# Scatter of the pair that went ahead, moved between the two gate and up products of an expert pair

## The chip, the cores and the metric

The kernel runs on one core of one Trainium2 chip. The metric is the device time of one execution in microseconds; three executions of the kernel before gave 1489.64, 1482.80 and 1488.08 us, median 1488.08 us.

## The reference

256 tokens of width 1024, all in float32, go through one layer of a first model (attention with rotary positions, a spatial gating unit, attention over 256 memory rows, a mixture of experts) and two layers of a second (stick-breaking attention and retention, each followed by a mixture of experts). The change lies in the three mixtures of experts alone. Each of them computes, cut to what matters:

```python
for e in range(16):
    he = silu(t @ w_gate[e]) * (t @ w_up[e])       # 256 x 1024 by 1024 x 512, twice
    y = y + combine[:, e:e + 1] * (he @ w_down[e]) # 512 x 1024
```

`combine` is zero for all but two experts of a token, so a kernel may compute for each expert only the tokens that chose it.

## The kernel before, in words

Five engines run their own programs and meet at semaphores. The matrix work is TensorE's, written in the order in which it is executed. In what follows the three mixtures of experts are called layers 0, 1 and 2.

**Tiling of a layer.** Each expert gets 64 slots (`CAP`) for tokens. Four experts form a quad: `gather_quad` fills their 256 slots by products with a 0/1 matrix `SELQ` that DVE makes. Two experts form a pair, worked on together: the even one sits in rows 0 to 63, the odd one in rows 64 to 127. A layer has 8 pairs, p = 0 to 7, p = 2q + k for quad q and half k. Pairs 0, 1, 6 and 7 are written out; pairs 2 to 5 are two rounds of a loop over q.

**A pair on TensorE (function `pair`, from line 927).** In this order:
1. `gate_up` for the even expert (a = 0): 16 products of 64 x 512 with `w_gate` and `w_up`; then the same for the odd expert (a = 1). Each waits for its two weight panels (`landed`), and for `ye`, the count of finished output halves of the pair ahead.
2. k = 0: `turn_pair_slots` twice, which turns `SELQ` for both pairs of the quad. k = 1: first half of `gather_quad` for the next quad.
3. `turn_h`: four transposes of the hidden rows `HH`, after ACT's silu (line 1533) and DVE's product (line 2195) for the odd expert (`h`). ACT copies the turned rows into `HT` (line 1563), which `ht` counts.
4. `down_half` for output columns 0 to 511, the other half of `gather_quad` where k = 1, `down_half` for columns 512 to 1023.
5. `more`: if an expert has over 64 tokens, a further block of 64 with products of its own (lines 994 and on). Its branch is passed twice in each pair.

**The scatter.** After `down_half`, ACT and DVE weight an output half and split it into a high and a low part, `YH` and `YL` (`ye` counts them). `scatter_before(h)` of the next pair adds column half h of the pair that went ahead into four accumulators: 4 products of 128 x 512 with the turned selection `SELTS`. A pair has two, so 8 products. It waits for `ye` and for `swt`, ACT's copies of the turned selection. The second one counts up `moe_scat`; before `YH`, `YL` and one of the selections are written anew, ACT and DVE wait for that. In the kernel before, where k = 0, `scatter_before(0)` stands between the turns of the slots and `turn_h`, and `scatter_before(1)` behind `turn_h`; where k = 1, both stand behind `turn_h`. Pair 0 of a layer has none (`first`), and the last pair's own output is scattered at the end of the layer.

**The weights.** Each expert has three panels of 2 MB (`w_gate`, `w_up`, `w_down`). A ring of six slots holds one pair's six panels: `ring_lo` for the even expert, `ring_hi` for the odd one. SyncE issues the loads (`load_expert`, line 1211) for the next pair, in this order: gate and up of the even expert, gate and up of the odd one, down of the even one, down of the odd one. Each waits until the slot has been read: gate and up until that expert's `gate_up` has ended, down until the pair's `down_half` has. All loads go through one queue.

Of the kernel before, what the change touches and what calls it, by code (L numbers as in the profile page):

```python
# [100 lines left out]
def build(nc, A, out, stop, final_ready):  # L101
# [7 lines left out]
    def S(name):  # L109
        if name not in sems:  # L110
            sems[name] = ctx.enter_context(nc.semaphore(name))
        return sems[name]
# [304 lines left out]
    def _(pe):  # L417
# [341 lines left out]
        def moe(L):  # L759
# [167 lines left out]
            def pair(q, k, first=False, final=False):  # L927
# [18 lines left out]
                if k == 0 and not first:  # L946
                    wait_moe(pe, L, "xe_a", 2 * q + 2)
                    wait_moe(pe, L, "xe_v", 2 * q + 2)
                for a in range(2):
                    if not first:  # L950
                        wait_moe(pe, L, "ye", 2 * p - 1 + a)
                    for j in range(2):
                        pe.wait_ge(landed[s[a][j]], 16 * p + at[a][j])
                    lo = P * k + CAP * a
                    gate_up(banks[a], lambda c: XE[:, c, lo:lo + CAP], wg[a], wu[a], S("moe_gu"), a == 0,
                            chunks_in if first and a == 0 else None)
                    if first and a == 0 and L:
                        pe.wait_ge(S("diag"), 2 * L)
                        for h in range(2):
                            ins = mm(ps[:, (B_XG, B_TR)[h], :], cst(C_ONES), GB[:, h * 512:(h + 1) * 512], True, True)  # L960
                        ins.then_inc(S("gate_sum"), 1)
                if k == 0:
                    if first:
                        pe.wait_ge(S("turner_in"), 2 * L + 2)
                        if L:
                            pe.wait_ge(S("gate_in"), L)
                    turn_pair_slots(0)
                    turn_pair_slots(1)
                    if not first:
                        scatter_before(0)  # L970
                elif not final:
                    wait_moe(pe, L, "sel", q + 2)
                    wait_moe(pe, L, "swt", 2 * q + 2)
                    wait_moe(pe, L, "ws", 2 * q + 2)
                    gather_quad(0)
                wait_moe(pe, L, "h", 2 * p + 2)
                turn_h(banks[0])
                if k == 1:
                    scatter_before(0)
                if not first:  # L980
                    scatter_before(1).then_inc(S("moe_scat"), 1)
                wait_moe(pe, L, "ht", p + 1)
                for a in range(2):
                    pe.wait_ge(landed[s[a][2]], 16 * p + at[a][2])
# [1608 lines left out]
```

## Time and profile before

| | us |
|---|---|
| median of three runs | 1488.08 |
| lowest and highest | 1482.80, 1489.64 |
| the profiled execution's own time | 1482.80 |
| its span, first to last instruction | 1480.9 |
| TensorE matmul busy | 1320.8 (89%) |
| DVE, ACT, POOL busy | 581.3, 431.7, 410.2 |
| DMA bytes, mean rate | 448.04 MB, 303 GB/s |
| mean granted TensorE clock | 0.968 of full speed |

A timeline row gives the start of a group of instructions within the span, how long it lasted, engine, line, tiles, shape and count, and in brackets how long the engine sat idle before it and what ended that. "issue" means that the profile shows no other instruction that it waited for. All products are made in one helper, line 419; which product a row is, its tiles tell: `ring_lo` or `ring_hi` with `Z` x32 is a `gate_up` of the even or the odd expert (the trace has two entries for each of the 16 products), `TURN,SELQ` the turns of slots, `YHS,SELTS` and `YLS,SELTS` the scatter, line 884 `turn_h`, and `ring_lo` alternating with `ring_hi` a `down_half`. The layers lie at about 289 to 521 us (layer 0), 697 to 962 us (layer 1) and 1214 to 1468 us (layer 2) of the span.

### The profile page before, as it was taken

How to read it: one execution, taken by the hardware profiler on the slowest of the kernel's cores; microseconds unless marked ns; L12 is line 12 of the kernel's file. 1: busy time of each engine (PE TensorE's matmuls, PEld its weight loads, DVE VectorE, ACT ScalarE, POOL GpSimd, SP SyncE). 2: the span in 40 equal slices, each digit the busy share in tenths (PEclk: the TensorE clock that was granted, in tenths of full speed). 3: DMA queues.
4: the chain of work that ended last, by engine and by line, in shares of the span. 5: the costliest groups of instructions: out<-in, count | busy, mean ns of one | idle time of the engine just before them, and what ended most of it. 6: DMA issues, size and time to landing. Idle time of an engine off the chain costs nothing.

```text
span 1480.9 us, 20887 instructions
## 1 busy us (share of the span) xinstructions
PE 1320.8 (89%) x7694; PEld 815.7 (55%) x7695; DVE 581.3 (39%) x1234; ACT 431.7 (29%) x693; POOL 410.2 (28%) x190
## 2 busy tenths in 40 slices
PE   7999987889899889998789799789997979889975
PEld 6886775534334389766234334279886853333422
DVE  5598543612112162447214222279007062322224
ACT  4554433211111146443111111145435331111110
POOL 5892643100000067151000000069964710000000
PEclk9999999999999999999899999999999999999998
DMA  7664566999999975518589999976544479999953
GB/s 285 215 201 173 186 228 231 393 402 426 426 428 428 391 283 183 190 58 338 231 344 420 426 422 428 397 269 235 191 150 191 170 321 412 422 416 420 427 221 126
DMA packets 89628, 448.04 MB, mean 303 GB/s; under 512 B 7804, under 2 KB 9768, under 8 KB 70952
## 3 DMA queue, kind: packets, MB, share of 16 engines
q1 hardware_dynamic: 85856, 445.87, 75.4%
q8 instruction: 79, 1.29, 0.4%
q10 hardware_dynamic: 3656, 0.57, 0.3%
q14 instruction: 37, 0.30, 0.1%
HBM read 445.38 MB, written 1.05 MB: 301 GB/s over the span
## 4 chain that ended last, share of the span: by engine, by line
PE 65%; DMA 15%; DVE 9%; issue 4%; POOL 3%; ACT 3%; ACTq 0%; SPq 0%; DVEq 0%; POOLq 0%
PE ps L419 63%; DMA ring_hi<-in_moe_w_up 10%; DMA ring_hi<-in_w_up 3%; POOL WLO L2528 3%; DMA ring_hi<-in_ada_w 1%; ACT WHI L1326 1%; DVE Z L1944 1%; DVE Z L1932 1%; DVE Z L1945 1%; DVE Z L1943 1%; DMA ring_lo<-in_w_ckv 1%; PE ps L884 1%; DMA ring_lo<-in_ret_w_in 1%; DMA ring_lo<-in_w_out 1%; POOL RS L2497 1%
## 5 line engine op out<-in xcount | busy, mean ns | idle before, releaser
L2528 POOL TENSOR_TENSOR WLO<-ring_lo,WHI 128x1024 fp32r<-128x1024 f32 (+1 forms) x154 | 379.3, 2485 | 702.6 <-ACT WHI L1326 700.7
L419 PE MATMUL ps<-ring_hi,Z 128*64 128x512 f32 x1248 | 375.4, 616 | 25.3 <-DMA ring_hi<-in_moe_w_up 14.4
L419 PE MATMUL ps<-ring_lo,Z 128*64 128x512 f32 x1152 | 350.6, 613 | 33.6 <-issue 24.3
L419 PEld LDWEIGHTS ps<-ring_lo,Z 128*64 128x64 f32 x1152 | 111.0, 141 | 248.2 <-issue 234.1
L1326 ACT ACTIVATE WHI<-ring_lo 128x1024 fp32r<-128x1024 f32 (+1 forms) x160 | 165.5, 1048 | 214.1 <-PE ps L419 177.3
L419 PEld LDWEIGHTS ps<-ring_hi,Z 128*64 128x64 f32 x1248 | 119.6, 142 | 153.7 <-issue 147.5
L2195 DVE TENSOR_TENSOR Z<-ps,Z 64x512 f32<-64x512 f32 x48 | 33.1, 689 | 357.4 <-ACT Z L1533 354.2
L1533 ACT ACTIVATE Z<-ps 64x512 f32<-64x512 f32 x48 | 28.4, 591 | 370.4 <-PE ps L419 357.6
L419 PE MATMUL ps<-WHI,HTH 128*128 128x512 f32 x320 | 126.8, 396 | 7.2 <-POOL WLO L2528 3.2
L419 PE MATMUL ps<-WLO,HTH 128*128 128x512 f32 x320 | 125.1, 391 | 0.0
L419 PE MATMUL ps<-WHI,HTL 128*128 128x512 f32 x320 | 125.1, 391 | 0.0
L2497 POOL TENSOR_TENSOR RS<-MS,NEGH 128x1 f32<-128x1 f32 (+2 forms) x26 | 22.2, 856 | 357.8 <-DVE MS L1781 298.7
L419 PE MATMUL ps<-HTH,WHI 128*128 128x256 f32 x320 | 92.2, 288 | 6.6 <-POOL WLO L2528 4.0
L419 PE MATMUL ps<-HTL,WHI 128*128 128x256 f32 x320 | 91.2, 285 | 0.0
L419 PE MATMUL ps<-HTH,WLO 128*128 128x256 f32 x320 | 91.1, 285 | 0.0
L419 PEld LDWEIGHTS ps<-WHI,HTH 128*128 128x128 f32 x320 | 60.5, 189 | 22.5 <-issue 6.3
L419 PEld LDWEIGHTS ps<-WHI,HTL 128*128 128x128 f32 x320 | 60.4, 189 | 12.9
L419 PEld LDWEIGHTS ps<-WLO,HTH 128*128 128x128 f32 x320 | 60.5, 189 | 11.9
L419 PEld LDWEIGHTS ps<-HTH,WHI 128*128 128x128 f32 x320 | 62.1, 194 | 8.4 <-issue 5.0
L419 PEld LDWEIGHTS ps<-HTL,WHI 128*128 128x128 f32 x320 | 62.1, 194 | 0.0
L419 PEld LDWEIGHTS ps<-HTH,WLO 128*128 128x128 f32 x320 | 62.1, 194 | 0.0
L419 PE MATMUL ps<-SELQ,XSPLIT 128*128 128x256 f32 x288 | 50.7, 311 | 5.7 <-DVE SELQ L2144 5.7
(299 smaller groups left out, 1719.2 us busy)
## 6 DMA issues: line engine op xcount, KB each, us to landing
ring_lo<-in_ada_w SPq DMA_DIRECT2D x22, 2048.0 KB, 8.1
ring_lo<-in_moe_w_gate SPq DMA_DIRECT2D x16, 2048.0 KB, 12.1
ring_lo<-in_moe_w_up SPq DMA_DIRECT2D x16, 2048.0 KB, 16.5
ring_lo<-in_moe_w_down SPq DMA_DIRECT2D x16, 2048.0 KB, 12.6
ring_hi<-in_moe_w_gate SPq DMA_DIRECT2D x16, 2048.0 KB, 13.6
ring_hi<-in_moe_w_up SPq DMA_DIRECT2D x16, 2048.0 KB, 18.5
ring_hi<-in_moe_w_down SPq DMA_DIRECT2D x16, 2048.0 KB, 16.9
ring_lo<-in_ret_w_in SPq DMA_DIRECT2D x12, 2048.0 KB, 8.1
```

The source lines that it names most:

```text
L419: return nc.tensor.matmul(o, l, r, start=start, stop=stop, skip_group_check=True)
L884: ins = nc.tensor.transpose(ps[:, bank, c * P:(c + 1) * P], by4[:, c, :], ident)
L1326: nc.scalar.activation(WHI[:, q, 0:size], slot(r)[:, q * size:(q + 1) * size], Copy).then_inc(S("hi_split"), 1)
L1533: nc.scalar.activation(SG[r, :], ps[CAP - CAP * a:P - CAP * a, bank, :], ACT.Silu).then_inc(S("moe_sg"), 1)
L1932: ins = V.tensor_tensor(qk4[:, t, h], qk4[:, t, h], gain, ALU.mult)
L1943: V.tensor_tensor(t1, x0, c1, ALU.mult)
L1944: link(V.tensor_tensor(t2, x1, c2, ALU.mult))
L1945: link(V.tensor_tensor(o, t1, t2, op))
L2195: V.tensor_tensor(HH[r, :], ps[r, bank, :], SG[r, :], ALU.mult).then_inc(S("moe_h"), 1)
L2497: nc.gpsimd.tensor_tensor(RS[:, par, at:at + width], MS[:, par, at:at + width], NEGH[:, 0:width], ALU.pow).then_inc(S("rstd"), 1)
L2528: nc.gpsimd.tensor_tensor(WLO[:, q, 0:size], slot(r)[:, q * size:(q + 1) * size], WHI[:, q, 0:size].bitcast(F32), ALU.subtract).then_inc(S ...
```

## The change

Both calls of `scatter_before` now stand between the `gate_up` of the even and of the odd expert, in each pair but the first. Nothing is added or taken away.

```diff
                 for a in range(2):
+                    if a and not first:
+                        scatter_before(0)
+                        scatter_before(1).then_inc(S("moe_scat"), 1)
                     if not first:
                         wait_moe(pe, L, "ye", 2 * p - 1 + a)
                     for j in range(2):
...
                     turn_pair_slots(0)
                     turn_pair_slots(1)
-                    if not first:
-                        scatter_before(0)
                 elif not final:
...
                 wait_moe(pe, L, "h", 2 * p + 2)
                 turn_h(banks[0])
-                if k == 1:
-                    scatter_before(0)
-                if not first:
-                    scatter_before(1).then_inc(S("moe_scat"), 1)
                 wait_moe(pe, L, "ht", p + 1)
```

TensorE's program in the loop, k = 0 (pairs 2 and 4), before; `landed3` and `landed4` are the odd expert's gate and up panels, `CST,Z` is `turn_h`:

```order
L419 MATMUL ps<-ring_lo,Z 64x512 x15
L953 REGISTER_ALU [waits moe_ye]
L419 MATMUL ps<-ring_hi,Z 64x512 [waits landed4,landed3]
L419 MATMUL ps<-ring_hi,Z 64x512 x15
L419 MATMUL ps<-TURN,SELQ 128x160 x4
L419 MATMUL ps<-YHS,SELTS 128x512 [waits moe_swt,moe_ye]
...
L884 MATMUL ps<-CST,Z 128x128 [waits moe_h]
L884 MATMUL ps<-CST,Z 128x128 x3
L419 MATMUL ps<-YHS,SELTS 128x512 [waits moe_swt,moe_ye]
...
L419 MATMUL ps<-ring_lo,Z 64x512 [waits landed5,landed1,moe_ht]
```

The same place after the change:

```order
L419 MATMUL ps<-ring_lo,Z 64x512 x15
L419 MATMUL ps<-YHS,SELTS 128x512 [waits moe_swt,moe_ye]
...
L956 REGISTER_ALU [waits moe_ye]
L419 MATMUL ps<-ring_hi,Z 64x512 [waits landed4,landed3]
L419 MATMUL ps<-ring_hi,Z 64x512 x15
L419 MATMUL ps<-TURN,SELQ 128x160 x4
L884 MATMUL ps<-CST,Z 128x128 [waits moe_h]
L884 MATMUL ps<-CST,Z 128x128 x3
L419 MATMUL ps<-ring_lo,Z 64x512 [waits landed5,landed1,moe_ht]
```

All eight scatter products now stand ahead of the odd expert's `gate_up`, and none stands beside the waits for `h` and `ht`.

TensorE's program of pair 1, k = 1 (its `gather_quad` is `SELQ,XSPLIT`), before:

```order
L419 MATMUL ps<-ring_hi,Z 64x512 [waits landed4,landed3,moe_ye]
...
L419 MATMUL ps<-SELQ,XSPLIT 128x256 [waits moe_ws,moe_swt,moe_sel]
...
L884 MATMUL ps<-CST,Z 128x128 [waits moe_h]
L884 MATMUL ps<-CST,Z 128x128 x3
L419 MATMUL ps<-YHS,SELTS 128x512 [waits moe_swt,moe_ye]
...
L419 MATMUL ps<-ring_lo,Z 64x512 [waits landed5,landed1,moe_ht]
```

And after the change:

```order
L419 MATMUL ps<-YHS,SELTS 128x512 [waits moe_swt,moe_ye]
...
L419 MATMUL ps<-ring_hi,Z 64x512 [waits landed4,landed3,moe_ye]
...
L419 MATMUL ps<-SELQ,XSPLIT 128x256 [waits moe_ws,moe_swt,moe_sel]
...
L884 MATMUL ps<-CST,Z 128x128 [waits moe_h]
L884 MATMUL ps<-CST,Z 128x128 x3
L419 MATMUL ps<-ring_lo,Z 64x512 [waits landed5,landed1,moe_ht]
```

Here the gather still stands beside the wait for `h`; beside the wait for `ht` nothing is left.

## Rows read from the trace of the kernel before

**Rows 1.** The page's chain of waits, shares of the span by engine.
```profile
PE 65%; DMA 15%; DVE 9%; issue 4%; POOL 3%; ACT 3%; ACTq 0%; SPq 0%; DVEq 0%; POOLq 0%
```

**Rows 2.** A stretch of layer 0: length, busy per engine, clock, DMA share, GB/s.
```profile
298.00:508.00 210.00, 190.04 (x886) 79.20 (x882) 39.47 (x116) 29.98 (x56) 0.00 (x0) 0.97 1.00 424
```

**Rows 3.** Timeline of TensorE, layer 0, pair 0, which has no scatter.
```profile
303.17 0.68 PE L419 MATMUL ps<-TURN,SELQ 128*128 128x160 f32 x4
304.67 0.75 PE L884 MATMUL ps<-CST,Z 128*128 128x128 f32 x4 [0.82 <-DVE Z L2195]
306.10 0.64 PE L419 MATMUL ps<-ring_lo,Z 128*64 128x512 f32 x1 [0.69 <-ACT Z L1563]
```

**Rows 4.** Timeline of TensorE, layer 0, pair 2 (k = 0).
```profile
359.87 0.68 PE L419 MATMUL ps<-TURN,SELQ 128*128 128x160 f32 x4
...
362.96 0.64 PE L419 MATMUL ps<-ring_lo,Z 128*64 128x512 f32 x1
```

**Rows 5.** Timeline of TensorE, layer 0, pair 5 (k = 1).
```profile
449.80 0.65 PE L884 MATMUL ps<-CST,Z 128*128 128x128 f32 x4
450.20 0.48 PE L419 MATMUL ps<-YHS,SELTS 128*128 128x512 f32 x1
...
452.21 0.64 PE L419 MATMUL ps<-ring_lo,Z 128*64 128x512 f32 x1
```

**Rows 6.** Timeline of ACT, the same pair: the copy of the turned rows.
```profile
450.72 0.60 ACT L1563 ACTIVATE Z<-ps 128x512 f32<-128x512 f32 x1
```

**Rows 7.** Timeline of TensorE, layer 2, pair 7, the last.
```profile
1454.52 0.75 PE L884 MATMUL ps<-CST,Z 128*128 128x128 f32 x4 [1.43 <-DVE Z L2195]
...
1457.04 0.64 PE L419 MATMUL ps<-ring_lo,Z 128*64 128x512 f32 x1
```

**Rows 8.** Timeline of TensorE, layer 2: starts of the products of pairs 2, 3, 5 and 6.
```profile
1272.20 8.79 PE L419 MATMUL ps<-ring_lo,Z 128*64 128x512 f32 x32 [4.69 <-issue]
...
1301.59 9.79 PE L419 MATMUL ps<-ring_lo,Z 128*64 128x512 f32 x32 [3.54 <-issue]
...
1365.02 7.09 PE L419 MATMUL ps<-ring_hi,Z 128*64 128x512 f32 x32 [1.06 <-DMA ring_hi<-in_moe_w_up]
...
1386.20 7.09 PE L419 MATMUL ps<-ring_lo,Z 128*64 128x512 f32 x32 [0.39 <-issue]
1394.96 7.09 PE L419 MATMUL ps<-ring_hi,Z 128*64 128x512 f32 x32 [1.67 <-DMA ring_hi<-in_moe_w_up]
```

**Rows 9.** Timeline of TensorE, layer 0: products of pairs 5 and 7.
```profile
439.06 8.78 PE L419 MATMUL ps<-ring_hi,Z 128*64 128x512 f32 x32 [2.79 <-DMA ring_hi<-in_w_up]
...
488.01 7.09 PE L419 MATMUL ps<-ring_lo,Z 128*64 128x512 f32 x32 [1.95 <-DMA ring_lo<-in_w_up]
...
497.90 8.78 PE L419 MATMUL ps<-ring_hi,Z 128*64 128x512 f32 x32 [2.80 <-DMA ring_hi<-in_w_up]
```

**Rows 10.** Timeline of TensorE, layer 1: products of pairs 3, 5, 6 and 7.
```profile
819.03 8.73 PE L419 MATMUL ps<-ring_hi,Z 128*64 128x512 f32 x32 [2.71 <-DMA ring_hi<-in_moe_w_up]
...
880.04 7.09 PE L419 MATMUL ps<-ring_hi,Z 128*64 128x512 f32 x32 [0.94 <-DMA ring_hi<-in_moe_w_up]
...
909.41 7.09 PE L419 MATMUL ps<-ring_hi,Z 128*64 128x512 f32 x32 [1.09 <-DMA ring_hi<-in_moe_w_up]
...
928.98 7.09 PE L419 MATMUL ps<-ring_lo,Z 128*64 128x512 f32 x32 [2.39 <-DVE YLS L2209]
938.75 8.60 PE L419 MATMUL ps<-ring_hi,Z 128*64 128x512 f32 x32 [2.68 <-DMA ring_hi<-in_moe_w_up]
```

**Rows 11.** Timeline of SyncE: issue of layer 1's last panel, start and duration of the issue.
```profile
927.12 0.33 SPq L1211 DMA_DIRECT2D ring_hi<-in_moe_w_down  x1
```

**Rows 12.** DMA issues, window 926.6 to 928: KB each, us from issue to landing.
```profile
ring_hi<-in_moe_w_down SPq DMA_DIRECT2D x1, 2048.0 KB, 22.9
```

**Rows 13.** Timeline of TensorE, layer 2, the further block of pair 6.
```profile
1416.15 1.13 PE L860 MATMUL ps<-CST,XROWS 128*128 128x128 f32 x4 [1.58 <-ACT XROWS L1583]
1419.48 8.87 PE L419 MATMUL ps<-ring_hi,Z 128*64 128x512 f32 x32 [2.20 <-DVE Z L2186]
```

## The prediction

> **What bounds the kernel now.** I read the chain of waits first. It is TensorE for 65% of the span and DMA for 15% [rows 1]. So the order on TensorE counts, but a part of its time in the layers of experts is waiting for weights. Next I read stretches of the layers. From 298 to 508 us the DMA engines are busy all the time, at 424 GB/s [rows 2]. A pair's six panels are 12.58 MB; at 424 GB/s that is 29.7 us per pair. The third view is TensorE's timeline in a pair. There the two work at nearly the same pace: TensorE waits 0.9 to 2.8 us for a panel in some pairs [rows 8 to 10] and not at all in the others. A step that TensorE gains or loses in such a layer is therefore taken up by the next wait for a panel, as long as there is one, and reaches the end of the layer only behind the last such wait. I cost the change in each pair first, and then walk through the waits of each layer.
>
> **What the scatter costs where it now stands.** Eight products start at 450.20 and the next thing starts at 452.21 [rows 5]: 2.0 us with the change of weights, of which I count 1.9. Between the two `gate_up` nothing hides it, unless the odd expert's panel is late. The scatter itself waits for nothing there: its `ye` was reached before or soon after the pair began, and its `swt` in the pair ahead.
>
> **What it gives back where it stood.** Its old place hid waits, and that cover is now gone.
> - k = 0, pairs 2, 4, 6. From the turns of the slots to the first down product takes 3.09 us with the scatter [rows 4]. Pair 0 has no scatter, and needs 2.93 us: it sits idle 0.82 us for DVE's product and 0.69 us for ACT's copy instead [rows 3]. So the scatter was hidden but for 0.16 us. Taken with 1.9 us ahead, such a pair gets 1.7 us longer.
> - k = 1 with a gather, pairs 1, 3, 5. The gather covers the wait for DVE. `turn_h` starts at 449.80, the down product at 452.21, 2.41 us later [rows 5]. ACT's copy ended at 450.72 + 0.60 = 451.32 [rows 6], so without the scatter it could start at 451.37, 0.8 us sooner. Such a pair gets 1.9 - 0.8 = 1.1 us longer.
> - Pair 7 has no gather, and ACT has nothing else to do. From `turn_h` to the down product takes 2.52 us [rows 7]; in pair 0 it takes 1.43 [rows 3]. It gives back 1.1 us and gets 0.8 us longer.
>
> If TensorE never waited for a panel, a layer would get 3 x 1.7 + 3 x 1.1 + 0.8 = 9.2 us longer. Now the waits.
>
> **A gain beside it: the clock.** Behind an idle time of 2.79 us a `gate_up` took 8.78 us, behind one of 1.95 us it took 7.09 [rows 9]; the granted clock fell in the first and not in the second. With the scatter in the idle time of 2.8 us, 0.9 us of it is left, and the 1.7 us should be saved. A wait of 2.8 us thus absorbs 2.8 + 1.7 = 4.5 us of shift.
>
> **Layer 2.** Pairs 1 to 4 are not held up by panels. Pairs 2 and 3 begin with idle times of 4.69 and 3.54 us put down to issue [rows 8], which I leave as they are. When the odd expert's products of pair 5 should start, the shift is 1.1 + 1.7 + 1.1 + 1.7 + 1.9 = 7.5 us, less 1.06 us of waiting [rows 8]: 6.4. Pair 5 gives back 0.8: 5.6. Pair 6 adds 1.9 and has 1.67 us of waiting to give [rows 8]: 5.9. From here no panel is waited for: the further block of pair 6 and the panels of pair 7 follow TensorE's pace. Pair 6 gives back 0.2, pair 7 adds 0.8. Layer 2: **+6.5 us**. Do the panels come later as well? SyncE issues them at TensorE's pace, up to 5.6 us later; but when the odd expert's products begin, the pair's two down panels are still in the queue, 4.2 MB or some 10 us at 424 GB/s (an estimate from rows 2), so few of these microseconds reach the landings. I bound them by 0 and 3 us, and up to 3 us changes nothing, since TensorE is later than that.
>
> **Layer 0.** Pairs 1 to 4 shift by 5.6 us. Pair 5 adds 1.9 and its wait takes 4.5 [rows 9]: 3.0; less 0.8: 2.2. Pair 6: 3.9. Pair 7 begins with a wait of 1.95 us [rows 9], of which 0.4 are the pause that a pair begins with where nothing holds it up (0.39 at pair 6 of layer 2) [rows 8]: 2.35. It adds 1.9, and the wait of 2.80 with the clock takes 4.5 [rows 9]: its products end 0.25 us sooner than before. It gives back 1.1. Layer 0: **-1.4 us**.
>
> **Layer 1.** Pairs 1 and 2 shift by 2.8. Pair 3 adds 1.9, and its wait with the clock (2.71 + 1.6) takes 4.3 [rows 10]: 0.4; less 0.8: -0.4. Pair 4: 1.3. Pair 5 adds 1.9, waits 0.94 less, gives back 0.8: 1.4. Pair 6 adds 1.9, waits 1.09 less, gives back 0.2: 2.0. Pair 7's first products wait 2.39 us, 2.0 of them to give [rows 10]: 0. The scatter goes into the wait of 2.68 us, and the odd expert's products end 1.5 us sooner for the clock [rows 10]. With 1.1 given back the down product could start 2.6 us sooner than at 951.3, but its last panel lands at 927.12 + 22.9 = 950.0 [rows 11, 12]. So 1.2 us sooner. TensorE then has been idle 1.4 us, busy 0.75 and idle about 2: the pattern of the further block (idle 1.58, busy 1.13, idle 2.20), after which the products took 8.87 us in place of 7.1 [rows 13]. I take that here too: 1.6 us lost. Layer 1: **+0.4 us**, between -1.2 and +0.4.
>
> **The sum** is 6.5 - 1.4 + 0.4 = +5.5 us. The profiled execution took 1482.80 us, the lowest of three, and would take 1488.3; on the median of 1488.08 it gives 1493.6. No other stage is touched; DVE, ACT and SyncE get the same work, and the later `moe_scat` only comes earlier in the pair.
>
> **Rivals.**
> - *The short idle times lower the clock (slower).* Each pair with k = 0 now idles twice for 0.7 to 0.85 us within 2.3 us, and pair 7 idles 1.4 and 0.7. If the clock fell each time, each would lose 1.7 us: pairs 2, 4, 6 and 7 of layer 2 give 6.8, pair 7 of layer 0 1.7, the rest goes into waits. +5.5 + 8.5 = +14.0: 1502.1. It decides from the second such pair on, since 5.5 + 1.7 = 7.2 is still within the bound. Against it: in pair 0 the same two idle times (0.82, 0.69) lowered nothing [rows 3]. The Trainium skill (TensorE: Matmul & The Clock Gate, A second HAM failure mode: psum-queue depth-cycling) tells of a kernel in which short idle times between groups of products made the clock swing between its two levels; by that rule this rival is what happens, and the trace of pair 0 does not agree.
> - *The stalls put down to issue come at other places (slower or faster).* They stand only behind the branch over the further blocks: 4.69 and 3.54 us in layer 2, with 1.7 and 2.7 us of low clock behind them [rows 8]. If the shifted program meets one more uncovered stall of this size in layer 2, it costs 4.7 + 1.7 = 6.4: +11.9, 1500.0. If instead both shrink to the usual 0.4 us, layer 2 has 7.4 + 4.4 = 11.8 us less on TensorE. Pairs 5 and 6 then wait for their panels as before, the shift at pair 6 is 0, and layer 2 gives only -0.2 + 0.8 = +0.6; the sum is -0.4: 1487.7. The Trainium skill (Runtime: NRT & Kernel Launch, Instruction fetch mechanics) says that a taken branch out of the fetched window makes the engine wait for a block of instructions. By that rule the stalls hang on where the branches lie, and those have not moved; no row here names the fetch.
> - *The waits take up more than I walked (no change).* Where layer 2's shift is smaller because the panels, not TensorE, set pairs 5 and 6, it is the case above. I count it there.
> - *Faster by over 0.5%.* It would need 7.4 us. The clock saved once per wait of 2.7 to 2.8 us gives 1.7 us at four places [rows 9, 10], 6.8 in all, most of it taken back by the later panels. I see no row for more.
>
> **How the numbers follow.** About 0.5%, 7.4 us, is what a measurement of this kernel can tell from no change. My forecast, +5.5 with some 2.5 us of uncertain shift, has a chance of 0.60: 0.50 of it within the bound, 0.10 over it. The clock rival has 0.10, all slower. One more stall has 0.10, slower. Shorter stalls or panels that set the pace have 0.16, within the bound. Faster has 0.04. Together: faster 0.04, same 0.66, slower 0.30. The likeliest time is 1493.6. The range reaches down to the case without shift in layer 2, less the spread of a median (the three runs lie within 6.8 us): 1485.5. It reaches up to one more stall and a microsecond: 1501.0.
>
> **What would show it.** In the profile after, the odd expert's products should start 1.9 us behind the even one's in pairs 1 to 4 of each layer, with `YHS,SELTS` rows in between. The turns of the slots should be followed by idle times near 0.8 and 0.7 us, and `turn_h` in k = 1 by about 0.8 us. The waits of 2.7 to 2.8 us on panels should be gone or under 1 us, the products behind them at 7.1 us in place of 8.8. Pair 6 of layer 2 should no longer wait for its panel. Layers 0 and 1 should end within 1.5 us of before, layer 2 some 6 us longer. I would be wrong if down products behind the new idle times took over 8 us, if the pauses between pairs changed, or if TensorE in layer 2 still waited for panels.

## The result, and the profile after

The changed kernel is slower. Its median of four runs is 1507.99 us (1503.69 to 1514.35); four runs of the kernel before gave 1486.13 (1482.80 to 1489.64). The ratio is 1.015, with a 95% interval of 1.0105 to 1.0196. The forecast of 1493.6 us was too low by 14.4, and 1507.99 lies outside the range of 1485.5 to 1501.0. A second set of four runs of the changed kernel gave 1506.20 and a ratio of 1.0132 (1.0098 to 1.0167). So the change costs some 20 us of 1486, and 5.5 were forecast.

The page of the changed kernel, of an execution of 1507.19 us:

```profile
PE 1341.0 (89%) x7694; PEld 816.8 (54%) x7695; DVE 580.8 (39%) x1234; ACT 431.0 (29%) x693; POOL 410.1 (27%) x190
...
PE 73%; DVE 9%; DMA 7%; ACT 4%; issue 4%; POOL 2%; ACTq 0%; SPq 0%; DVEq 0%; POOLq 0%
```

The last line answers to [rows 1]. DMA's share of the chain fell from 15% to 7%, and TensorE's rose from 65% to 73%. The waits for weights are mostly gone, as forecast, but what took their place is longer than they were. TensorE has the same 7694 entries of products in the trace and is busy for 1341.0 us with them; before it was 1320.8. The same products taking 20 us longer is the first sign of a lower clock. Only a sign, since the two traces are not average ones: the execution profiled before was the shortest of its runs, with a clock of 0.968, where the means of the later runs of the same kernel are 0.962 to 0.964.

The second view is one row for each of the three layers of experts, from the first product of the first gather to the last scatter. The columns are: stretch, length, busy time and count of PE, of PEld, DVE, ACT and POOL, mean granted TensorE clock, DMA share, GB/s. Before:

```profile
283.30:521.10 237.80, 215.84 (x1012) 93.64 (x1014) 51.33 (x154) 34.62 (x65) 0.00 (x0) 0.96 0.99 415
691.30:961.90 270.60, 236.93 (x1091) 101.13 (x1091) 73.70 (x190) 38.61 (x72) 0.00 (x0) 0.96 0.91 383
1207.50:1467.60 260.10, 234.12 (x1091) 98.77 (x1091) 72.56 (x184) 38.61 (x72) 0.00 (x0) 0.96 0.86 359
```

After:

```profile
282.60:524.40 241.80, 217.23 (x1012) 92.63 (x1016) 51.46 (x154) 36.08 (x67) 1.14 (x1) 0.97 0.99 411
693.80:969.00 275.20, 241.87 (x1091) 100.72 (x1091) 73.68 (x190) 38.28 (x72) 0.00 (x0) 0.94 0.90 376
1213.30:1492.10 278.80, 246.38 (x1091) 100.50 (x1091) 72.62 (x184) 38.28 (x72) 0.00 (x0) 0.93 0.80 335
```

Layer 0 is 4.0 us longer where -1.4 was forecast, layer 1 is 4.6 longer (+0.4), layer 2 is 18.7 longer (+6.5). The granted clock is the column to look at. Length x (1 - clock) is the most that the clock can cost there; it counts idle time at the lower level too, which costs nothing. In layer 2 that is 260.1 x 0.04 = 10.4 us before and 278.8 x 0.07 = 19.5 after, in layer 1 it is 10.8 and 16.5, in layer 0 9.5 and 7.3. Each row is one execution, and a layer's clock moves from one execution to the next: in the trace of the kernel with pair 7 alone changed, further down, layer 2 has 0.93 as well. What the clock costs is therefore taken from means over runs, in the experiments. DMA's share in layer 2 fell from 0.86 to 0.80: the weights had more time than they needed.

The third view is TensorE's waits, over the whole program (engine, tile, line, what ended the wait: us in total, times, longest). Before:

```profile
PE ps L419 <- issue: 31.4, 15, 5.1
PE ps L419 <- DMA ring_hi<-in_moe_w_up: 14.4, 7, 4.2
...
PE ps L884 <- DVE Z L2195: 6.8, 6, 1.4
```

After:

```profile
PE ps L419 <- issue: 34.1, 15, 5.3
PE ps L419 <- ACT Z L1560: 20.8, 24, 1.3
PE ps L884 <- DVE Z L2192: 14.4, 15, 1.4
```

The 24 waits for ACT are one per pair, ahead of the first down product; before there were three, 2.1 us in all. Nine waits for DVE, ahead of `turn_h`, are new: the pairs with k = 0 but the first, three in each layer. The waits put down to issue are 15 as before.

For layer 2, in these two traces, this closes the account. Its busy time grew by 246.38 - 234.12 = 12.3 us and its idle time by 32.42 - 25.98 = 6.4, together 18.7. Of the idle time, +9.1 are waits for ACT and DVE, -2.7 waits for panels. Of the busy time, I take 9.6 us for clock: by the clock's records, products ran for 17.5 us at the lower level before and for 36.7 after, and half of such time is lost. Not all of it is the change's work, as the count of single falls below shows. 2.7 us are left that no row names; a part is the seam between the two `gate_up`, which takes 2.15 us more where I had counted 1.9.

### The single places

TensorE's timeline after (start, duration, engine, line, operation, output and inputs, count, idle time before it and what ended it). Layer 0, pair 2, which answers to [rows 4]; the end of its pair 5, which answers to [rows 5]; and pair 1 of layer 2:

```profile
365.44 0.68 PE L419 MATMUL ps<-TURN,SELQ 128*128 128x160 f32 x4
366.93 0.75 PE L884 MATMUL ps<-CST,Z 128*128 128x128 f32 x4 [0.81 <-DVE Z L2192]
368.36 0.64 PE L419 MATMUL ps<-ring_lo,Z 128*64 128x512 f32 x1 [0.69 <-ACT Z L1560]
...
455.18 0.65 PE L884 MATMUL ps<-CST,Z 128*128 128x128 f32 x4
456.76 0.64 PE L419 MATMUL ps<-ring_lo,Z 128*64 128x512 f32 x1 [0.93 <-ACT Z L1560]
...
1263.67 0.65 PE L884 MATMUL ps<-CST,Z 128*128 128x128 f32 x4
1265.43 0.64 PE L419 MATMUL ps<-ring_lo,Z 128*64 128x512 f32 x1 [1.11 <-ACT Z L1560]
```

The idle times of the k = 0 pairs are the 0.81 and 0.69 that pair 0 had [rows 3]. From `turn_h` to the down product pair 5 takes 1.58 us, as forecast; pair 1 of layer 2 takes 1.76. There the pair gives back 0.65 and not 0.8, since ACT's copy comes later.

The price of the seam, in pair 1 of layer 0, even expert's products to odd expert's products; before:

```profile
345.98 7.09 PE L419 MATMUL ps<-ring_lo,Z 128*64 128x512 f32 x32 [0.30 <-issue]
352.89 1.03 PE L419 MATMUL ps<-ring_hi,Z 128*64 128x512 f32 x4
```

And after:

```profile
349.35 7.09 PE L419 MATMUL ps<-ring_lo,Z 128*64 128x512 f32 x32 [0.26 <-issue]
358.42 1.08 PE L419 MATMUL ps<-ring_hi,Z 128*64 128x512 f32 x4
```

From start to start it is 6.91 us before and 9.07 after.

Where the clock fell in layer 2, by windows (columns as above): pair 2's down products, pair 6's down products, the further block, pair 7's down products. Before:

```profile
1290.96:1297.96 7.00, 7.00 (x33) 2.21 (x32) 3.70 (x13) 1.01 (x2) 0.00 (x0) 1.00 0.99 421
1405.06:1412.06 7.00, 7.00 (x35) 2.43 (x36) 3.10 (x12) 1.01 (x2) 0.00 (x0) 1.00 0.99 419
1419.48:1428.35 8.87, 8.87 (x32) 2.64 (x32) 0.00 (x0) 0.00 (x0) 0.00 (x0) 0.79 0.00 0
1457.04:1464.10 7.06, 7.06 (x33) 2.21 (x32) 1.45 (x2) 0.63 (x1) 0.00 (x0) 1.00 0.01 2
```

After:

```profile
1301.60:1308.60 7.00, 6.91 (x26) 2.27 (x28) 3.00 (x12) 0.87 (x2) 0.00 (x0) 0.76 1.01 431
1421.60:1428.60 7.00, 6.97 (x26) 2.23 (x28) 2.46 (x12) 0.88 (x2) 0.00 (x0) 0.76 0.63 264
1437.30:1447.30 10.00, 9.56 (x32) 2.74 (x32) 0.03 (x1) 0.31 (x1) 0.00 (x0) 0.74 0.00 0
1479.80:1488.00 8.20, 8.20 (x32) 2.59 (x32) 1.44 (x2) 0.63 (x1) 0.00 (x0) 0.79 0.01 2
```

In three of the four, down products that ran at full clock before (32 trace entries or more in 7 us) now do 26 entries in 7 us, or 32 in 8.2. The fourth, the further block, ran at a low clock before too. In front of each stand two short idle times: 0.89 and 0.76 us, 0.81 and 0.69, 1.42 and 0.69. But in pair 2 of layer 0 the same 0.81 and 0.69 cost nothing: its down products ran at full clock. So the two idle times alone do not decide it.

### The profile page after: what moved, and what is told of

Read it like the earlier page. It is cut to its first block, busy times and chain, and to the rows that moved or that the text cites. A ratio compares the mean times of both kernels' runs of the same rounds, so it can differ in the third digit from the quotient of the medians.

```text
span 1505.4 us, 20887 instructions
## 1 busy us (share of the span) xinstructions
PE 1341.0 (89%) x7694; PEld 816.8 (54%) x7695; DVE 580.8 (39%) x1234; ACT 431.0 (29%) x693; POOL 410.1 (27%) x190
## 3 DMA queue, kind: packets, MB, share of 16 engines
HBM read 445.38 MB, written 1.05 MB: 297 GB/s over the span
## 4 chain that ended last, share of the span: by engine, by line
PE 73%; DVE 9%; DMA 7%; ACT 4%; issue 4%; POOL 2%; ACTq 0%; SPq 0%; DVEq 0%; POOLq 0%
PE ps L419 71%; POOL WLO L2525 2%; DMA ring_lo<-in_ada_w 2%; DMA ring_hi<-in_moe_w_up 1%; DMA ring_hi<-in_w_up 1%; DMA ring_hi<-in_ada_w 1%; ACT Z L1560 1%; DVE Z L1941 1%; DVE Z L1929 1%; DVE Z L1942 1%; DVE Z L1940 1%; DMA ring_lo<-in_w_ckv 1%; PE ps L884 1%; DVE Z L2192 1%; DMA ring_lo<-in_w_out 1%
## 5 line engine op out<-in xcount | busy, mean ns | idle before, releaser
L419 PE MATMUL ps<-ring_lo,Z 128*64 128x512 f32 x1152 | 361.7, 627 | 48.0 <-issue 25.2
L419 PE MATMUL ps<-ring_hi,Z 128*64 128x512 f32 x1248 | 383.1, 623 | 10.3 <-DVE Z L2183 4.4
L419 PEld LDWEIGHTS ps<-ring_hi,Z 128*64 128x64 f32 x1248 | 115.5, 143 | 135.2 <-issue 129.2
## 6 DMA issues: line engine op xcount, KB each, us to landing
ring_lo<-in_moe_w_down SPq DMA_DIRECT2D x16, 2048.0 KB, 10.2
ring_hi<-in_moe_w_down SPq DMA_DIRECT2D x16, 2048.0 KB, 14.4
```

Of the source, the lines that this page charges most:

```text
L419: return nc.tensor.matmul(o, l, r, start=start, stop=stop, skip_group_check=True)
```

## The experiments

The time of a run says little about its cause, so I take two numbers for each kernel, both means over its runs. **Lost** is span x (1 - mean granted clock), what the clock takes. It counts idle time at the lower level too, so it is an upper measure. **Rest** is span x clock, all else: work, waits, order. The kernels were run in four sets on three chips, each set with runs of the kernel before on the same chip, for which lost was 53.9 to 56.3 us and rest 1429.5 to 1430.7. The first runs of the changed kernel stand outside these sets. The standard error of a mean of lost (its likely distance from the true mean) is at most 1.7 us, but 2.5 for the zeros in k = 1 and 3.6 for the first runs of the changed kernel.

| kernel | median us | ratio (95% interval) | lost | rest |
|---|---|---|---|---|
| changed kernel, first runs | 1508.0 | 1.015 (1.0105 to 1.0196) | 64.8 | 1441.9 |
| changed kernel, again | 1506.2 | 1.0132 (1.0098 to 1.0167) | 60.2 | 1443.7 |
| only k = 1 changed | 1494.7 | 1.0048 (1.002 to 1.0075) | 56.7 | 1435.3 |
| only k = 0 changed | 1490.7 | 1.0029 (1.0008 to 1.0049) | 55.1 | 1434.0 |
| scatter at both places | 1484.9 | 0.999 (0.9966 to 1.0015) | 43.8 | 1439.2 |
| half in front, k = 1 | 1484.7 | 0.9991 (0.9969 to 1.0014) | 52.4 | 1431.4 |
| changed, one scatter product | 1492.7 | 1.0041 (1.0012 to 1.0069) | 65.6 | 1425.3 |
| before, k = 0 uncovered | 1485.5 | 1.0002 (0.9974 to 1.003) | 54.3 | 1429.5 |
| before, k = 1 uncovered | 1486.8 | 0.9999 (0.9978 to 1.002) | 58.8 | 1426.4 |
| changed, zeros in all idle times | 1495.1 | 1.004 (1.002 to 1.006) | 46.1 | 1447.3 |
| changed, zeros in k = 1 | 1502.6 | 1.0106 (1.0048 to 1.0163) | 61.1 | 1438.8 |
| only pair 7 changed | 1487.8 | 1.0002 (0.9974 to 1.0029) | 55.7 | 1430.2 |
| before, zeros added | 1489.4 | 1.0031 (1.0011 to 1.0052) | 51.5 | 1436.8 |
| half in front, zeros added | 1489.4 | 1.0015 (0.9995 to 1.0035) | 47.8 | 1439.5 |

The two rows of the changed kernel, eight runs, give lost 62.5 and rest 1442.8. Against 54.1 and 1430.7 before, in the set that holds the second row, that is +8.4 us of clock and +12.1 us of order and waits. The second row alone gives +6.0 and +13.0.

### The two kinds of pairs apart

Only the pairs with k = 1 changed:

```diff
                 for a in range(2):
+                    if a and k == 1:
+                        scatter_before(0)
+                        scatter_before(1).then_inc(S("moe_scat"), 1)
...
-                if k == 1:
-                    scatter_before(0)
-                if not first:
+                if k == 0 and not first:
                     scatter_before(1).then_inc(S("moe_scat"), 1)
```

> The scatter is moved in the pairs with k = 1 only. Theory S (the order alone: TensorE pays about 2.15 us between the two products and gets 0.5 to 0.8 back): layer 2 gains 1.6 us in each of pairs 1, 3 and 5 and 1.1 in pair 7, less 2.7 us of waiting for panels, about +3 us; layers 0 and 1 between -2 and +1; ratio 1.000 to 1.003. Theory C (half of the loss is low clock behind the new idle times, which come above all with k = 0): nearly the same here, at most 3 us more, ratio up to 1.005.

Only the pairs with k = 0 changed, the same edit with `k == 0 and not first` in front, and k = 1 as before:

> The scatter is moved in the pairs with k = 0 only (pairs 2, 4, 6). Theory S: 2.15 us in each of three pairs of layer 2, less 2.7 us of waiting, about +4 us there, layers 0 and 1 near 0; ratio 1.002 to 1.004. Theory C: the down products of pair 2 or 6 and the further block of pair 6 in layer 2 run partly at the low level as well, 3 to 8 us more; ratio 1.005 to 1.009, and down products of some pair with k = 0 take over 8.5 us in place of 7.1.

The ratios are 1.0048 and 1.0029, rest rises by 5.2 and 3.9 us. The second ratio lies where the order alone was expected to put it, the first above that. In the account of the whole change that leaves 12.1 - 9.1 = 3.0 us of rest and 8.4 - 4.0 = 4.4 us of clock to neither half: +2.8 us and +1.2 us alone, +8.4 together. The standard error of these 4.4 us is some 3, so the halves do not show by themselves that the clock loses more than their sum. The halves also show where the new idle times come from. TensorE's waits, k = 1 alone:

```profile
PE ps L419 <- ACT Z L1564: 14.1, 15, 1.3
...
PE ps L884 <- DVE Z L2196: 6.8, 6, 1.4
```

And k = 0 alone:

```profile
PE ps L884 <- DVE Z L2195: 14.4, 15, 1.4
...
PE ps L419 <- ACT Z L1563: 8.7, 12, 0.9
```

All the new waits for DVE come with k = 0, and 12 of the 21 new waits for ACT with k = 1.

### The cover kept

The scatter in front, and again at its old places, with `moe_scat` counted once:

```diff
+                    if a and not first:
+                        scatter_before(0)
+                        scatter_before(1)
```

> The change, and the scatter is also left at its old places, so each pair's part is added twice (that is what it computes otherwise). TensorE has 8 more products per pair, 2.15 us in front and none of the new idle times. Theory S: slower than the changed kernel, since nothing is given back: about +25 us, ratio 1.016 to 1.020. Theory C: the low clock behind the turns and the down products is gone, which saves more than the second scatter costs: +13 to +18 us, ratio 1.009 to 1.012, and down products of all pairs at 7.1 us.

The time, 0.999 of before, lies below what either theory had. Lost fell to 43.8, rest rose by 9. But the doubled parts changed the activations from layer to layer, and with them the routing: layer 2 had no further block. A block's clock loss and time are missing from it, so this run is no evidence on the clock. The kernels with zeros below fill the idle times without touching the activations.

### Half in front

For k = 1, `scatter_before(0)` in front and `scatter_before(1)` left behind `turn_h`; k = 0 as before:

```diff
+                    if a and k == 1:
+                        scatter_before(0)
...
-                if k == 1:
-                    scatter_before(0)
                 if not first:
                     scatter_before(1).then_inc(S("moe_scat"), 1)
```

> Where k = 1, only column half 0 of the scatter stands between the two products and half 1 stays behind turn_h, where it covers ACT's copy; where k = 0 all stays as before. Theory S: 1.1 us in front, 1.0 us back behind turn_h: no shift where no panel is waited for; where one is, 1 us hides in the wait. Ratio 0.998 to 1.000. Theory C: the waits of 2.7 to 2.8 us become 1.7, so the clock does not fall behind them (1.7 us at four places): ratio 0.997 to 0.999.

0.9991 (0.9969 to 1.0014): no difference that could be measured. Four products behind `turn_h` are enough for ACT's copy, and then it hardly matters where the other four stand. Nothing is to be had from the four in front either.

### The scatter's work taken out

The changed kernel with one product of the scatter's eight in front, and the kernel before with the scatter of one kind of pair cut to one product, so that their waits are bare or nearly so. For k = 1 that product stands in front; for k = 0 it stands behind `turn_h`, in the second of the two idle times, which is then 0.45 to 0.62 us where the changed kernel has 0.69 to 0.86:

```diff
+                def scatter_one():
+                    for h in range(2):
+                        wait_moe(pe, L, "ye", 2 * p - 1 + h)
+                    wait_moe(pe, L, "swt", p)
+                    return mm(acc[0], SELT_[1 - k][:, 0:P], YH[0], False, False)
```

> The changed kernel with 1 of the 8 scatter products of a pair, in the new place; the other 7 are left out of pairs 1 to 7, so most of the experts' parts are missing from the output. The idle times behind the turns and behind turn_h are those of the change. Theory S: 1.7 us less per pair than the change, until the panels bound the pair: ratio 0.999 to 1.003. Theory C: the idle times and the clock falls behind them stay: some 4 to 10 us on top, ratio 1.003 to 1.008, with down products over 8.5 us in some pairs.

> The kernel before, but where k = 0 one scatter product behind turn_h stands in place of all eight, so the parts scattered in pairs 2, 4 and 6 are missing from the output. Less work, with the idle times of the change behind the turns and turn_h of these pairs and nothing in front. Theory S: 0 to 0.2 us less per pair, ratio 0.999 to 1.000. Theory C: the kernel gets slower although it does less, by 2 to 8 us in layer 2, ratio 1.001 to 1.005.

> The kernel before, but where k = 1 one scatter product between gate_up of the even and the odd expert stands in place of all eight, so the parts scattered in pairs 1, 3, 5 and 7 are missing from the output. Idle times of about 1 us behind turn_h come in pairs 1, 3 and 5 and of 0.7 us in pair 7. Theory S: some 1.5 us of work less per such pair, part of it hidden anyway: ratio 0.996 to 1.000, time lost to the clock unchanged at 54 us. Theory C: 3 to 5 us more lost to the clock, which eats the gain: ratio 0.999 to 1.003.

This is the clearest separation. With seven of eight products gone from the changed kernel, rest falls from 1442.8 to 1425.3, below the kernel before. Lost stays at 65.6. The kernel does 147 products less than before and is still 0.4% slower, because of the clock. The bare waits are there as in the changed kernel:

```profile
PE ps L419 <- ACT Z L1565: 20.1, 23, 1.3
PE ps L884 <- DVE Z L2197: 14.4, 15, 1.4
```

With one kind of pair uncovered, lost does not move (k = 0: 54.3 against 54.5) or moves little (k = 1: 58.8 against 56.3). The work that is missing is not gained either: what TensorE no longer does becomes a wait. Lost rises by 11.2 us with both kinds uncovered and by 2.4 for the two kinds added up, a difference of 8.8 with a standard error of some 3. It is not shown that this needs both kinds together, since the k = 0 kernel has a product in one of its idle times; the count of single falls below says where they stand.

### Products of zeros in the idle times

The other way round: the changed kernel with its idle times filled. `add_zero` multiplies by a stretch of zeros of `WR2S` and adds the product to a bank that is in use, which changes nothing in it.

```diff
+            def add_zero(n):
+
+                mm(acc[0][0:16, 0:n], WR2S[:, 16 * KC:16 * KC + 16], cst(C_ID, n), False, False)
...
+                if k == 0 or final:
+                    add_zero(384)
                 wait_moe(pe, L, "h", 2 * p + 2)
                 turn_h(banks[0])
+                add_zero(512 if k == 1 and not final else 384)
```

> The changed kernel with one product that adds zeros (16 rows, 384 or 512 columns) in each idle time that the change opened: behind the turns with k = 0, ahead of turn_h in pair 7, and behind turn_h in all pairs. The output stays the reference's. Theory S (order alone): these products lie in idle times, so nothing changes or it is a little slower: ratio 1.014 to 1.018. Theory C (the idle times let the clock fall): the time lost to the low level, span x (1 - granted clock), falls from about 65 us to 54 us or less as in the kernel before, and the ratio to 1.006 to 1.009, which is what the order alone costs.

A second kernel has them only behind `turn_h` in the k = 1 pairs other than pair 7:

> The changed kernel with the product that adds zeros only behind turn_h of the pairs with k = 1 (not pair 7), where ACT's copy is waited for. Output as the reference's. Theory C with each idle time by itself: the pairs with k = 0 keep their clock falls, ratio 1.011 to 1.014. Theory C with idle times adding up over a pair's neighbourhood: covering the pairs with k = 1 is enough to keep the level, ratio 1.007 to 1.010. Theory S: 1.014 to 1.017.

In all idle times, the time falls to a ratio of 1.004 (1.002 to 1.006), below what both theories had, with 39 products (78 trace entries) more than the changed kernel issues. Lost is 46.1, which is 16 us below the changed kernel and 10 below the kernel before beside it (56.3). The rest is 1447.3, 4.5 us over the changed kernel: nothing was saved there. Pair 2 of layer 2, where the changed kernel's down products ran at 0.76, now shows:

```profile
1292.51 0.68 PE L419 MATMUL ps<-TURN,SELQ 128*128 128x160 f32 x4
1293.11 0.82 PE L419 MATMUL ps<-CST,WR2S 128*16 128x384 f32 x2
...
1294.07 0.74 PE L884 MATMUL ps<-CST,Z 128*128 128x128 f32 x4
1294.75 0.82 PE L419 MATMUL ps<-CST,WR2S 128*16 128x384 f32 x2
```

From the turns to `turn_h` it still takes 1.5 us, as long as with the idle time; the wait was only made busy. This shows the clock's share directly: same waits for others, same order, more work, and 16 us less lost. The changed kernel was not run on this chip. Each against the kernel before in its own set, the kernel with zeros loses 10 us less and the changed kernel, in its second runs, 6 us more. Zeros in the k = 1 pairs alone left lost at 61.1, with only four runs: no difference from the changed kernel that could be measured.

### Pair 7 alone

```diff
                 for a in range(2):
+                    if a and final:
+                        scatter_before(0)
+                        scatter_before(1).then_inc(S("moe_scat"), 1)
```

with the old calls left out for `final`.

> The scatter is moved in pair 7 alone, the last of each layer; all other pairs stay as before. Both theories: layers 0 and 1 end 1 to 2.5 us sooner, since the scatter and the clock are saved in the last wait for a panel, layer 2 ends 1 us later: ratio 0.997 to 0.999. If the layers' ends are set by something else than that wait: 1.000 or more.

1.0002 (0.9974 to 1.0029), where 0.997 to 0.999 was expected. One pair in each layer makes no difference that could be measured; the interval is some 4 us wide to each side, so a gain or a loss of a microsecond per layer is not excluded.

This kernel is also a control for single traces. Up to pair 7 its layers are those of before. Yet in its profiled execution, the longest of its ten, layer 2 ran at 0.93 as in the changed kernel:

```profile
1211.10:1480.00 268.90, 241.57 (x1091) 100.52 (x1091) 72.70 (x184) 38.61 (x72) 0.00 (x0) 0.93 0.83 347
```

### A version that beats both?

The kernel before loses 54 us to the clock itself. So I filled its own idle times, of pair 0, pair 7 and of the further blocks, with zeros, in the order of before and in that of the half in front:

```diff
+                if first or final:
+                    add_zero(384)
                 wait_moe(pe, L, "h", 2 * p + 2)
                 turn_h(banks[0])
+                if first:
+                    add_zero(384)
```

> The kernel before (scatter where it stood) with products that add zeros in idle times that it already had: behind the turns and turn_h of pair 0, ahead of turn_h of pair 7, and in the further block (behind its turned slots, its turned rows, its gate_up and its down products). Output as the reference's. Theory C: the further blocks' products run at 7.1 us in place of 8.4 to 10.1 and the time lost to the low level falls by 4 to 10 us: ratio 0.993 to 0.997. Theory S: 1.000 to 1.001.

> The same zero products, with half of the scatter between the two gate_up where k = 1 as in the half-front kernel. Theory C: as the one before, or 1 us less where a panel is waited for: ratio 0.992 to 0.997. Theory S: 0.999 to 1.000.

In the further blocks one or two such products of 512 columns stand behind each of four steps that come before a wait.

Both lost less to the clock (51.5 and 47.8 us against 54.1) and neither was faster: 1.0031 (1.0011 to 1.0052) and 1.0015 (0.9995 to 1.0035). Both lie above what both theories had. The gain is there: in neither trace does the clock fall in a further block, where the thirteen other traces have 10 to 31 us at the lower level. A further block of layer 1, whose 32 trace entries took 8.44 us in the kernel before, took 7.09 here.

It is given back at another place, in the waits put down to issue, first kernel:

```profile
PE ps L419 <- issue: 48.1, 16, 5.5
```

The second kernel has 47.3 us in 16; the thirteen traces without these products have 28 to 39, the kernel before 31.4 in 15. In the layers of experts alone the first has 42.6 us against 26.3 before, and they stand at other places. Twenty-one products (42 trace entries) were added. Whether they shift the program against the points at which it stalls, or the stalls have another cause, was not tried by itself. I have no version that beats the kernel before.

### The changed kernel again

> The changed kernel again, on the same chip as these. Both theories: ratio 1.012 to 1.018. Theory C: of its 20 to 24 us, 8 to 13 are a difference in the time lost to the low clock level, span x (1 - granted clock), and the rest, span x granted clock, is 10 to 13 us longer.

1.0132, with lost 60.2 and rest 1443.7: 6.0 us more lost, less than the 8 to 13 that Theory C expected, and 13.0 us more rest. In its trace the layers ran at 0.97, 0.93 and 0.94; in the first it was 0.97, 0.94 and 0.93. Layer 2:

```profile
1215.30:1491.60 276.30, 244.27 (x1091) 100.32 (x1091) 72.47 (x184) 38.28 (x72) 0.00 (x0) 0.94 0.81 338
```

The layers' lengths repeat within 3 us. The single falls do not all repeat: pair 6's down products took long again, but pair 2's, at 0.76 of full clock in the first run, took 7.09 us.

**Where the clock falls, counted over the fifteen traces.** The clock's records give the start of each fall. Counted here are those that start between `turn_h` and the first 2 us of the down products behind it.

| idle times of a pair | pairs | with a fall |
|---|---|---|
| 0.8 to 0.9 us ahead of `turn_h` and 0.7 to 0.9 behind it, pairs 2, 4, 6 | 45 | 17 |
| 1.4 us ahead and 0.7 or more behind, pair 7 | 21 | 12 |
| 0.8 to 0.9 us ahead and 0.7 behind, pair 0 | 36 | 4 |
| 0.8 to 0.9 us ahead and 0.45 to 0.62 behind, pairs 2, 4, 6 | 9 | 1 |
| none ahead, 0.9 to 1.3 us behind, pairs 1, 3, 5 | 45 | 0 |
| 1.4 us ahead, none behind, pair 7 | 15 | 0 |

A fall stands behind two idle times in close succession, in about four of ten such pairs where the change makes them, and behind none of the 60 single ones. So the single idle times that the change opens in the pairs with k = 1 are not where it falls. With twelve pairs of the first two kinds, the changed kernel's two traces have five falls and four; at 1.7 us each, that is 7 to 8.5 us. Against that stand the four falls behind waits for panels of 2.7 to 2.8 us [rows 9, 10], which neither trace has any more: 6.8 us. The two together, 0 to 1.7 us, are less than the 6.0 to 8.4 us by which the mean of lost rose, and what makes up the difference is open.

## Why the prediction was wrong, point by point

**What bounds the kernel: right.** TensorE's part of the chain grew by what DMA's shrank. Waits for panels in the three layers fell from 8.4, 11.6 and 2.7 us to 0.7, 4.2 and 0 (sums of the rows of the waits in each layer). Pair 6 of layer 2 no longer waits for its panel.

**What the pairs cost: the mechanism right, the sizes too small.** In front it is 2.15 us and not 1.9. The pairs of k = 1 with a gather give back 0.8 us in layer 0, but 0.5 to 0.65 in layers 1 and 2; those of k = 0 give back 0.16 in layer 0 and about 0.1 in the others. So a layer that never waits for a panel gets 3 x 2.05 + 3 x 1.55 + 1.05 = 11.9 us longer, where I had 9.2. Over the whole program this step was nearly right: without its clock terms (four savings of 1.5 to 1.7 us and one loss of 1.6, -4.9 in all) the forecast of +5.5 is +10.4 us of order and waits, and rest rose by 12.1. Most of the difference reached the end in layer 2 alone, where nothing absorbs it.

**The clock: the step that failed.** "A wait of 2.8 us thus absorbs 2.8 + 1.7 = 4.5 us of shift" took the clock as a gain only. That part held at all four waits of 2.7 to 2.8 us. At the end of layer 0, [rows 9] had 8.78 us behind a wait of 2.80; after the change it reads

```profile
502.21 7.09 PE L419 MATMUL ps<-ring_hi,Z 128*64 128x512 f32 x32 [0.70 <-DMA ring_hi<-in_w_up]
```

Layer 0 did lose less to the clock than before. But I costed the many new short idle times at nothing. The evidence I gave was the one instance of pair 0 [rows 3], where two of them cost nothing. It is true, and I read it as a rule. Even for pair 0 it is none. The half-front kernel leaves pair 0 as it was, with the same 0.82 and 0.69 us in layer 0, and in its trace the clock fell there. The first 7 us of the down products, with 26 trace entries where the kernel before has 32:

```profile
305.41:312.41 7.00, 7.00 (x26) 2.28 (x28) 3.00 (x12) 0.89 (x2) 0.00 (x0) 0.76 1.01 432
```

The runs show the price of such idle times in every pair: 8.4 us more lost, where I had counted on 4.9 saved. That is 13.3 of the some 15 us by which the forecast was too low. The rival that had this mechanism got a chance of 0.10 and a price of 1502.1. It was right in kind, and wrong in saying that each such pair loses 1.7 us: of twelve, five and four did in the two traces.

Not every fall that is new in the trace after belongs to the change. In the further block of pair 0 in layer 1, 32 trace entries had taken 8.44 us and 16 of the next ones 3.65. After the change:

```profile
739.99 10.10 PE L419 MATMUL ps<-ring_hi,Z 128*64 128x512 f32 x32 [2.20 <-DVE Z L2183]
...
753.00 4.43 PE L419 MATMUL ps<-ring_hi,Z 128*64 128x512 f32 x12 [0.47 <-ACT Z L1587]
```

The 32 take 1.66 us longer, and only 12 of the others are done in 4.43 us. But the kernel with pair 7 alone changed, which has nothing changed ahead of this block in its layer, shows the same:

```profile
738.10 10.10 PE L419 MATMUL ps<-ring_hi,Z 128*64 128x512 f32 x32 [2.20 <-DVE Z L2189]
...
751.11 4.43 PE L419 MATMUL ps<-ring_hi,Z 128*64 128x512 f32 x12 [0.47 <-ACT Z L1593]
```

By the clock's records, the further blocks have 10.2 us at the lower level in the trace before and 23.9 in the trace after. The other traces that have both blocks, with no zeros in them, have 17 to 31, eleven traces with the one after. So the trace before was a lucky one there, and 6.8 us of the difference between the two traces are luck and not the change.

The Trainium skill (TensorE: Matmul & The Clock Gate, A second HAM failure mode: psum-queue depth-cycling) tells of a kernel whose short idle times between groups of products made the clock swing between its two levels. By that rule the change loses to the clock, and the runs agree: 62.5 us against 54.1. In the prediction I set one instance of the trace above it. A rule on a pattern and one instance do not contradict each other.

**The panels of layer 0: wrong.** I walked the waits with the landings fixed: "up to 3 us changes nothing". In layer 0 the panels set the pace, and they came later. SyncE's last issue and its time from issue to landing (the columns of the second are KB and us), before:

```profile
486.60 1.43 SPq L1211 DMA_DIRECT2D ring_hi<-in_w_down  x1
...
ring_hi<-in_w_down SPq DMA_DIRECT2D x1, 2048.0 KB, 21.5
```

After:

```profile
493.14 0.33 SPq L1208 DMA_DIRECT2D ring_hi<-in_w_down  x1
...
ring_hi<-in_w_down SPq DMA_DIRECT2D x1, 2048.0 KB, 18.9
```

Issued 6.5 us later, it landed at 493.14 + 18.9 = 512.0 in place of 486.60 + 21.5 = 508.1, so 3.9 us later. The queue took up 2.6 us and no more. A ring slot comes free when TensorE has used it; so a later TensorE makes a later panel, and a wait for it is no fixed point in time. With the odd expert's products of pair 7 starting at 502.21 in place of 497.90, 4.3 us later, the rest follows: 1.7 less for the clock, 1.1 given back, and the last scatter waits longer:

```profile
522.30 0.47 PE L419 MATMUL ps<-YHS,SELTS 128*128 128x512 f32 x1 [3.08 <-issue]
```

It was 1.35 us before. 4.3 - 1.7 - 1.1 + 1.7 = 3.2, plus 0.7 for the earlier start of the layer: 3.9 of the 4.0 measured.

**Layer 1: wrong in the same two steps.** Its waits for ACT and DVE and the like grew by 7.0 us, nearly what its waits for panels shrank by, 7.4. But products ran for 27.7 us at the lower clock in place of 21.5, which is 3.1 us. The other 1.9 us to +4.6 no row names; the seams are a part. I had forecast 1.6 and 1.5 us saved at two waits and 1.6 lost at the end. The two savings came and the loss did not; what took their place is one fall behind new idle times, and more low clock in the further block and at one pause put down to issue, where the change has no part that I can show.

**Layer 2: right in its walk, wrong in its size.** TensorE was late at each pair and no panel was waited for. The +6.5 became +9.1 for waits of ACT and DVE, -2.7 for panels, +9.6 for the clock and +2.7 for the rest. Of the clock's part, three falls behind the new idle times, in pairs 2, 6 and 7, are some 5 us; the further block is most of the others.

**The stalls put down to issue: right.** They were left as they are, and in layer 2 they are 10.3 us in five before and 10.4 us in five after. The rival with one more stall did not happen, nor the one with shorter stalls.

**The chances: too narrow.** With 0.66 on no measurable difference, I had spread the uncertainty of the one cost that I could not read (the new idle times) over one rival and no range. It should have been bound from both sides like any unknown cost: nothing (pair 0), or 1.7 us for each of the 12 pairs of this kind in the three layers, 20.4 us on top of the sum; and the range would have held 1508.

**What stays open.** Why the clock falls behind two short idle times in one pair and not in the next. Pairs with the same two idle times run at either level, in one run and from run to run. Of the short idle times, the traces have falls only behind two in close succession, and the runs show that filling them ends the loss. Open are also the some 6 us of lost that the counted falls do not make up, and the 3.0 us of rest that belong to neither half.

## What to carry to other kernels

Work that stands beside a short wait hides the wait and also keeps TensorE busy; moved to where nothing waits, it costs twice, here 12 us in order and 8 us of clock for the same products. Before such a move, count the idle times that it bares over the whole stage, above all two close together, and bound the price of each such place by the lower level of the clock, even where the trace has one that cost nothing. And take what the clock costs from several executions: a layer that nothing had changed up to its last pair ran at 0.96 in one trace and at 0.93 in another. And do not take the landings of a saturated queue as fixed when it is the late engine that frees the buffers.

## What was unexpected of the hardware

Two idle times of 0.7 to 1.4 us in close succession let the clock fall in 29 of 66 pairs of experts where the change or a variant of it made them, and a single one of 0.9 to 1.4 us in none of 60. With them in all pairs, 6 to 11 us more were lost to the clock. Products of zeros in the same idle times brought the clock above that of the kernel before: 46.1 us lost against 56.3. And 21 added products of zeros, which saved 2.6 us of clock, came with 16.7 us more of waits put down to issue.
